# Stick-breaking attention by two sigmoids and a running product, with the scores read from PSUM

## What is computed

```python
z = jnp.einsum('bhqd,bhkd->bhqk', q_blk, kh).astype(jnp.float32) * inv_sqrt
mask = key_pos[None, :] < q_pos[:, None]
log_1m_beta = jnp.where(mask, jax.nn.log_sigmoid(-z), 0.0)
suffix = lax.cumsum(log_1m_beta, axis=3, reverse=True) - log_1m_beta
a = jnp.where(mask, jnp.exp(jax.nn.log_sigmoid(z) + suffix), 0.0)
return jnp.einsum('bhqk,bhkd->bhqd', a, vh.astype(jnp.float32)).astype(q.dtype)
```

## Time and profile before

| | us |
|---|---|
| median of three runs | 3073.14 |
| lowest, highest | 3069.12, 3074.96 |
| profiled execution | 3063.84 |
| its span | 3062.1 |
| stage of this attention, from 1864 to 2102 us | 238 |
| in it, PE, DVE and ACT busy | 200.3, 195.5, 137.0 |

### The profile page before, as it was taken

How to read it: one execution, slowest core, us unless ns; L and a number is a source line. 1 busy time by engine, 2 the same in 40 slices (tenths; PEclk the granted TensorE clock), 3 DMA queues, 4 the chain that set the end, 5 groups by cost and what they waited for, 6 DMA issues and landing times.

```text
span 3062.1 us, 42914 instructions
## 1 busy us (share of the span) xinstructions
PE 2875.2 (94%) x16394; PEld 2321.4 (76%) x16394; DVE 1624.6 (53%) x2005; ACT 752.3 (25%) x1421; POOL 1058.9 (35%) x746
## 2 busy tenths in 40 slices
PE   7998898979899999999799999879998999999997
PEld 6886567868788888888678886657876888888886
DVE  3464544662677777777732005884134455445545
ACT  3323564323311111101420004563124001100111
POOL 4321001348534333333643322112358333323333
PEclk9998999999999999999899999999999999999999
DMA  3200000013222222222221111001131111111111
GB/s 123 55 27 11 10 6 22 3 48 133 69 89 77 81 82 85 87 82 82 83 69 45 51 35 35 15 1 56 55 124 56 55 41 55 48 48 43 53 49 61
DMA packets 213435, 172.12 MB, mean 56 GB/s; under 512 B 15543, under 2 KB 188878, under 8 KB 213326
## 3 DMA queue, kind: packets, MB, share of 16 engines
q1 hardware_dynamic: 160670, 135.47, 14.3%
q10 hardware_dynamic: 52656, 35.13, 3.8%
HBM read 162.19 MB, written 8.39 MB: 56 GB/s over the span
## 4 chain that ended last, share of the span: by engine, by line
PE 82%; DVE 8%; POOL 4%; issue 2%; ACT 2%; DMA 1%; SPq 0%; DVEq 0%; ACTq 0%; POOLq 0%
PE ps L873 13%; PE ps L875 13%; PE ps L874 13%; PE ps L1290 7%; PE ps L1291 7%; PE ps L1292 7%; PE ps L1082 2%; PE ps L1000 2%; DVE sb_weights L2476 1%; PE ps L892 1%; PE ps L894 1%; PE ps L893 1%; POOL rstd L666 1%; PE ps L1022 1%; POOL slab_lo L240 1%
## 5 line engine op out<-in xcount | busy, mean ns | idle before, releaser
L237 POOL TENSOR_SCALAR slab_hi<-raw 128x1024 fp32r<-128x1024 f32 (+1 forms) x236 | 263.4, 1116 | 1540.4 <-PE ps L875 581.1
L240 POOL TENSOR_TENSOR slab_lo<-raw,slab_hi 128x1024 fp32r<-128x1024 f32 (+1 forms) x236 | 576.8, 2444 | 19.7
L873 PE MATMUL ps<-act_hi,slab_hi 128*128 128x512 f32 x1472 | 575.2, 391 | 2.0 <-DVE act_lo L1986 1.6
L875 PE MATMUL ps<-act_hi,slab_lo 128*128 128x512 f32 x1472 | 572.9, 389 | 0.0
L874 PE MATMUL ps<-act_lo,slab_hi 128*128 128x512 f32 x1472 | 572.7, 389 | 0.0
L2391 DVE TENSOR_TENSOR acc<-ps,acc 128x512 f32<-128x512 f32 x512 | 339.5, 686 | 200.6 <-PE ps L1292 200.5
L1290 PE MATMUL ps<-slab_hi,hid_hi 128*128 128x512 f32 x1024 | 403.4, 394 | 4.2 <-POOL acc L794 2.5
L1291 PE MATMUL ps<-slab_hi,hid_lo 128*128 128x512 f32 x1024 | 399.5, 390 | 0.0
L1292 PE MATMUL ps<-slab_lo,hid_hi 128*128 128x512 f32 x1024 | 399.3, 390 | 0.0
L1813 ACT ACTIVATE relu<-ps 128x512 f32<-128x512 f32 x128 | 77.0, 602 | 1041.2 <-PE ps L875 1023.1
L873 PEld LDWEIGHTS ps<-act_hi,slab_hi 128*128 128x128 f32 x1472 | 276.4, 188 | 59.8 <-DVE act_lo L1986 1.7
(11 more groups left out here) (320 smaller groups left out, 4252.9 us busy)
## 6 DMA issues: line engine op xcount, KB each, us to landing
raw<-in_w_in SPq DMA_DIRECT2D x56, 512.0 KB, 3.8
w_ada<-in_w_ada ACTq DMA_DIRECT2D x48, 512.0 KB, 4.1
raw<-in_w_out SPq DMA_DIRECT2D x32, 512.0 KB, 3.4
raw<-in_w_up SPq DMA_DIRECT2D x32, 512.0 KB, 4.1
raw<-in_w_down SPq DMA_DIRECT2D x32, 512.0 KB, 3.2
raw<-in_w_mlp_in SPq DMA_DIRECT2D x32, 512.0 KB, 4.1
raw<-in_w_mlp_out SPq DMA_DIRECT2D x32, 512.0 KB, 3.3
x_tok<-in_x SPq DMA_DIRECT2D x8, 512.0 KB, 6.2
```

The costliest lines, as they stand in the source:

```text
L237: pool.tensor_scalar(self.hi[s][:, 0:width], self.raw[r][:, 0:width], 1.0, 0.0, ALU.mult, ALU.add)\
L240: pool.tensor_tensor(self.lo[s][:, 0:width], self.raw[r][:, 0:width], self.hi[s][:, 0:width].bitcast(F32), ALU.subtract).then_inc(self.spl ...
L873: pe.matmul(o, hi[:, w], a_hi[:, k, cols], start=(k == 0), stop=False)
L875: mm = pe.matmul(o, lo[:, w], a_hi[:, k, cols], start=False, stop=(k == nk - 1))
```

## The change

The weights are computed as products instead of by logarithms. ACT reads the scores from PSUM twice: sigmoid(z) into sb_weights and sigmoid(-z) into a new tile sb_rest (two buffers, in the place of sb_z). DVE forms the running product of sb_rest from the last key to the first, and multiplies sb_weights by it, shifted by one key. The copies of the scores by DVE go. DVE adds -1e30 (0 below the diagonal) to the 128 columns on the diagonal, in place in PSUM, for both items of a tile behind the weights of an even item. The banks of the scores are free when ACT has read them (sb_beta_done). The turned weights are copied, without an exp. On PE the scores of the next tile move behind the transposes of item s - 2. The table of functions of ACT is another one, which has Tanh too.

```diff
@@ PE
-                pe.wait_ge(sem("sb_z_copied"), SB_ITEMS * i + 2 * t + 2)
+                pe.wait_ge(sem("sb_beta_done"), SB_ITEMS * i + 2 * t + 2)
...
-                    if s % 2 and s + 1 < SB_ITEMS:
-                        sb_scores(i, s // 2 + 1)
                     if s % 2 == 0 and s < 12 and not last:
                         sb_project(i + 1, s // 3, SB_THIRDS[s % 3])
                     if s % 2 == 0 and (late := lagged(i, before, s, SB_LAG_PV, SB_ITEMS)):
                         sb_outputs(late[0], late[1] // 2)
                     if late := lagged(i, before, s, SB_LAG_TURN, SB_ITEMS):
                         sb_turn(*late)
+                    if s % 2 and s + 1 < SB_ITEMS:
+                        sb_scores(i, s // 2 + 1)
                     if s % 2 and s < 12 and not last:
                         sb_project(i + 1, s // 3, SB_THIRDS[s % 3])
...
-            pe.wait_ge(sem("sb_z_copied"), SB_ITEMS * SB_PAIRS + 2)
+            pe.wait_ge(sem("sb_beta_done"), SB_ITEMS * SB_PAIRS + 2)
@@ ACT
-            act.preload_act_table_set("natural_log_exp_and_others")
+            act.preload_act_table_set("sigmoid_and_others")
...
-            def sb_softplus(i, s, before):
-                n = (s // 2 + 1) * P
-                z, l = sb_z[s % 2][:, 0:n], sb_w[s % SB_SLOTS][:, 0:n]
-                act.wait_ge(sem("sb_z_copied"), SB_ITEMS * i + s + 3)
+            def sb_betas(i, s, before):
+                n, at = (s // 2 + 1) * P, SB_ITEMS * i + s
+                z = ps[:, 2 * (s % 2):2 * (s % 2) + 2, :].rearrange("p b n -> p (b n)")[:, 0:n]
+                act.wait_ge(sem("sb_masked"), at + 1)
                 if slot := lagged(i, before, s, SB_SLOTS, SB_ITEMS):
                     act.wait_ge(sem("sb_turned"), SB_GROUPS * slot[0] + (sb_groups(slot[1])[-1] + 1))
-                act.activation(l, z, ACT.Exp).then_inc(sem("sb_exp_done"), 1)
-                act.wait_ge(sem("sb_exp_done"), SB_ITEMS * i + s + 1)
-                act.activation(l, l, ACT.Ln, bias=1.0).then_inc(sem("sb_ln_done"), 1)
+                act.activation(sb_w[s % SB_SLOTS][:, 0:n], z, ACT.Sigmoid)
+                if at >= 2:
+                    act.wait_ge(sem("sb_arg_done"), at - 1)
+                act.activation(sb_rest[s % 2][:, 0:n], z, ACT.Sigmoid, scale=-1.0).then_inc(sem("sb_beta_done"), 1)
...
-                    act.activation(sb_at[g % 4][:, 0:w], ps[:, 4 + g % 2, 0:w], ACT.Exp).then_inc(sem("sb_at_done"), 1)
+                    act.copy(sb_at[g % 4][:, 0:w], ps[:, 4 + g % 2, 0:w]).then_inc(sem("sb_at_done"), 1)
@@ DVE
+            def sb_mask(i, s):
+                f, col = divmod(s // 2 * P, HALF)
+                diagonal = ps[:, 2 * (s % 2) + f, col:col + P]
                 dve.wait_ge(sem("sb_scores"), SB_ITEMS * i + s + 1)
-                if n > P:
-                    dve.tensor_scalar(z[:, 0:n - P], scores[:, 0:n - P], SB_Z_CAP, None, ALU.min)
-                dve.tensor_tensor(z[:, n - P:n], scores[:, n - P:n], key_cap, ALU.min).then_inc(sem("sb_z_copied"), 1)
...
+                dve.tensor_tensor(diagonal, diagonal, consts[:, C_KEYCAP:C_KEYCAP + P], ALU.add).then_inc(sem("sb_masked"), 1)
+
+            def sb_weights(i, s):
+                n, at = (s // 2 + 1) * P, SB_ITEMS * i + s
+                rest, w = sb_rest[s % 2], sb_w[s % SB_SLOTS]
+                dve.wait_ge(sem("sb_beta_done"), at + 3)
+                ch.link(dve.tensor_tensor_scan(rest[:, 0:n][:, ::-1], rest[:, 0:n][:, ::-1], rest[:, 0:n][:, ::-1], 1.0, ALU.mult, ALU.bypass))
+                dve.tensor_tensor(w[:, 0:n - 1], w[:, 0:n - 1], rest[:, 1:n], ALU.mult).then_inc(sem("sb_arg_done"), 1)
```

More of the change, by code:

```diff
@@ L65 @@
 SB_LAG_TURN, SB_LAG_PV = 2, 4
-SB_Z_CAP = 40.0
+SB_MASKED = -1e30
 def sb_groups(s):
@@ L167, in constants @@
         c[:, C_LEVEL + n * CHUNK:C_LEVEL + (n + 1) * CHUNK] = ((k[:, :CHUNK] // s) % 2 == 1) & (r % CHUNK // s == k[:, :CHUNK] // s - 1)
-    c[:, C_KEYCAP:C_KEYCAP + P] = np.where(k < r, SB_Z_CAP, -1e30)
+    c[:, C_KEYCAP:C_KEYCAP + P] = np.where(k < r, 0.0, SB_MASKED)
     c[:, C_ID64:C_ID64 + CHUNK] = r % CHUNK == k[:, :CHUNK]
@@ L431, in two_blocks @@
         k2 = [sb(f"k2_feat{i}", kb, [P, SEQ]) for i, kb in enumerate((21, 85))]
-        sb_z = [sb(f"sb_z{i}", 41 + 4 * i, [P, SEQ]) for i in range(2)]
+        sb_rest = [sb(f"sb_rest{i}", 41 + 4 * i, [P, SEQ]) for i in range(2)]
         sb_w = [sb(f"sb_weights{i}", kb, [P, SEQ]) for i, kb in enumerate((49, 53, 73, 77))]
@@ L652, in _ @@
             for name, credit in (("kk_prod", 1), ("o_taken", 1), ("o_ss_done", 1), ("ada_used", 2), ("ada_read", 1), ("c2_cg_read", 1), ("c2_v_done", 1), ("c2_y_done", 1),
-                                 ("m_gate_read", 2), ("m_done", 2), ("sb_z_copied", 2), ("sb_o_done", 2)):
+                                 ("m_gate_read", 2), ("m_done", 2), ("sb_beta_done", 2), ("sb_o_done", 2)):
                 pool.sem_inc(sem(name), credit)
@@ L1930, in sb_pair @@
                         sb_take_projection(i + 1, s // 3 - 1)
-                    sb_softplus(i, s, before)
+                    sb_betas(i, s, before)
                     if late := lagged(i, before, s, SB_LAG_TURN, SB_ITEMS):
@@ L2458, in _ @@
                         .then_inc(sem("m_done"), 1)
-            key_cap = consts[:, C_KEYCAP:C_KEYCAP + P]
-            def sb_cap_scores(i, s):
-                n = (s // 2 + 1) * P
-                z, scores = sb_z[s % 2], ps[:, 2 * (s % 2):2 * (s % 2) + 2, :].rearrange("p b n -> p (b n)")
+            def sb_mask(i, s):
+                f, col = divmod(s // 2 * P, HALF)
+                diagonal = ps[:, 2 * (s % 2) + f, col:col + P]
                 dve.wait_ge(sem("sb_scores"), SB_ITEMS * i + s + 1)
-                if n > P:
-                    dve.tensor_scalar(z[:, 0:n - P], scores[:, 0:n - P], SB_Z_CAP, None, ALU.min)
-                dve.tensor_tensor(z[:, n - P:n], scores[:, n - P:n], key_cap, ALU.min).then_inc(sem("sb_z_copied"), 1)
@@ L2472, in sb_log_weights @@
-            def sb_log_weights(i, s):
-                n = (s // 2 + 1) * P
-                z, l = sb_z[s % 2][:, 0:n], sb_w[s % SB_SLOTS][:, 0:n]
-                dve.wait_ge(sem("sb_ln_done"), SB_ITEMS * i + s + 1)
-                ch.link(dve.tensor_tensor_scan(l[:, ::-1], l[:, ::-1], l[:, ::-1], 0.0, ALU.add, ALU.bypass))
-                dve.wait_ge(sem("sb_z_copied"), SB_ITEMS * i + s + 3)
-                dve.tensor_tensor(l, z, l, ALU.subtract).then_inc(sem("sb_arg_done"), 1)
-                dve.wait_ge(sem("sb_arg_done"), SB_ITEMS * i + s + 1)
@@ L2481, in _ @@
-            sb_cap_scores(0, 0)
+                dve.tensor_tensor(diagonal, diagonal, consts[:, C_KEYCAP:C_KEYCAP + P], ALU.add).then_inc(sem("sb_masked"), 1)
[5 more added lines that the diff above has]
+                dve.tensor_tensor(w[:, 0:n - 1], w[:, 0:n - 1], rest[:, 1:n], ALU.mult).then_inc(sem("sb_arg_done"), 1)
@@ L2482, in _ @@
+            sb_mask(0, 0)
+            sb_mask(0, 1)
             for i in range(SB_PAIRS):
                 for s in range(SB_ITEMS):
-                    if s + 1 < SB_ITEMS:
-                        sb_cap_scores(i, s + 1)
-                    elif i + 1 < SB_PAIRS:
-                        sb_cap_scores(i + 1, 0)
-                    sb_log_weights(i, s)
+                    sb_weights(i, s)
+                    if s % 2 == 0:
+                        for h in range(2):
+                            if s + 2 < SB_ITEMS:
+                                sb_mask(i, s + 2 + h)
+                            elif i + 1 < SB_PAIRS:
+                                sb_mask(i + 1, h)
```

## The result

The changed kernel takes 3082.8 us (median of seven runs, 3077.7 to 3086.9); the kernel before, run beside it on the same chip, 3069.5 (3064.7 to 3075.0). The ratio is 1.004, with a 95% interval of 1.0027 to 1.0053 (8 to 16 us): slower by 13 us. The profiled executions are 3082.2 and 3063.8 us, 18 apart; that of the kernel before is shorter than all of its seven runs, so differences read from this pair of traces may be some us too large.

The account below looks back on a forecast made before the run. PE was taken to bound tiles 0 to 4 of a pair, DVE tiles 5 to 7 and the last pair. Stage +14.8, GpSimd 0.5 and clock 0.8 gave +16: 3089 us on the median, range 3075 to 3106.

Parts of the forecast that it names:

- The round trip: Attention tiles: PE transposes 2t-2, ACT copies it, ACT does two sigmoids, PE scores; stalls sum to 11.6 us a pair.
- Its price: Projecting pairs: stall per tile 0.99 us at t=1 growing to 2.34 at t=7, plus 1.2 for projection copies.
- The last pair: Last head pair, without projections: tile periods 3.6 to 7.5 us, about 37.0 against 41.1, so -4.1 us.
- The clock: TensorE's grant behind long waits at a pair's end: about +0.4 us for each of two boundaries, 0.8 in all.
- The clock rival: Projecting tiles: new stalls lower the grant, eight stretches, 32 us less half for what lies in stalls; 3105 us, chance 0.08.
- The stage: Stick-breaking attention: pairs +7.1, +6.1, +5.7 and -4.1 us, tail 0, sum +14.8.
- From the profiled time to the median: Whole kernel: +16 us on the profiled 3063.8 gives 3080, on the median 3073.1 gives 3089.
- slow scan: DVE's product scan at 1.5 times the adding scan exceeds the round trip in wide tiles: +13, 3102 us, chance 0.04.
- DVE's relief: Attention stage: 56 capped copies, 38.7 us, go; DVE is busy 30 to 35 us less and no longer bounds the first three pairs.
- The faster case: Attention pairs: the round trip is covered and only DVE's relief is left; -20 us, 3053, chance 0.06.
- T: PE's transposes of item 2t-1, the only PE work forecast to cover the round trip; 0.26 us at t=1, 0.92 at t=7.
- rival of half stalls: Attention tiles: the two sigmoids may overlap, stalls are half the sum, no change; about 3074 us, chance 0.10.

Follow-up runs that it names:

- e_act: Changed kernel with ACT doing both items' sigmoids of a tile first, then the copies of both turned items; 3071.3 us, ratio 1.0005 to the kernel before.
- e_proj: Changed kernel with the next pair's projections at odd items put ahead of the next tile's scores on PE; 3068.9 us, ratio 0.9995 to the kernel before.
- e_odd: Changed kernel with sigmoid(z) done twice for each odd item, 20.4 us more of ACT; 3117.8 us, ratio 1.0163 to the kernel before.
- e_even: Changed kernel with sigmoid(z) done twice for each even item, 20.4 us more of ACT; 3096.8 us, ratio 1.0092 to the kernel before.
- e_fill: Changed kernel with four spare matmuls before tile 5's scores in each projecting pair; median ratio 1.004 to the kernel before.
- e_dve: Changed kernel with 56 DVE reductions, 38.7 us, in the removed copies' widths, results unawaited; 3089.5 us, ratio 1.007 to the kernel before.
- e_outfill: Changed kernel with projections ahead of scores, outputs between a tile's transposes, and eight spare matmuls at item 13 of projecting pairs; 3062.0 us, ratio 0.9981 to the kernel before.
- e_back: Changed kernel with PE's order of the kernel before, scores ahead of the transposes of item 2t-1; 3112.4 us, ratio 1.0139 to the kernel before.
- e_bmove: Kernel before with only PE's new order, next tile's scores behind the transposes of item 2t-1; 3075.1 us, ratio 1.0014 to the kernel before.

## Why the prediction was right, and where its steps were off

Forecast were 3089 us and slower; it is 3083 and slower, by 13 us where 16 were forecast. The rest of the distance is the kernel before, whose median was 3073.1 us in the three runs that the forecast started from and 3069.5 in seven. Step by step:

- **The round trip** is the cause, as forecast. e_act takes ACT's copies out of it and e_proj puts PE's work under it; either removes the loss. e_odd against e_even shows that an activation costs over twice as much inside it as outside (16.9 us of idle PE against 7.2).
- **Its price** was well summed, but not as the steps had it. In the first pair PE's waits before the scores are 1.30, 1.02, 1.32, 1.93, 0.76, 0.97 and 0.54 us. Up to tile 5 they follow the forecast (0.99, 1.20, 1.42, 1.62, plus 0.6 twice for a projection's copy). Then they fall instead of growing beyond 2: an item of over 512 columns is turned in two groups, and PE waits for ACT's copies or for DVE between the transposes (0.66, 0.83 and 1.93 us), so part of the trip is paid there, though the kernel before had a wait of 2.4 us for DVE in the last of these places too. Together 11.3 us, where 12.8 were forecast; the waits before scores alone are 7.8, not the 9 to 12 that I had named as the sign.
- **Why less:** two activations in a row overlap, the two sigmoids of an item by 0.10 to 0.17 us, 0.12 in the mean of 64. In the timeline above they start 0.58 us apart and last 0.71. I had taken durations where the starts' distance counts, and allowed some 0.05. My remark that by the Trainium skill's figure the sum would move under 1 us was wrong. Put into the same steps, the figure of the Trainium skill (ScalarE: Activation LUTs, What ACT_TABLE_LOAD costs) adds 0.65 us to a projecting pair and 0.8 to the last, near 3 us in all (an estimate from the page's figure).
- **The last pair** was forecast at 37.0 and took 34.9. The periods from scores to scores at 384 to 1024 columns are 3.25, 4.08, 4.72, 5.56, 6.30 and 7.05 us, each 0.3 to 0.5 under the step's. Three to four such overlaps in a tile would give as much (an estimate; it was not tested apart).
- **The clock** is the mis-sized term. I gave it 0.4 us at each of two boundaries, 0.8 in all. The idle time of the projecting pairs was a little under the forecast, but PE's busy time rose by 3.3 (2.3 without the eight transposes that moved into the window), 2.6 and 2.0 us where I had added nothing but the 0.8. e_fill is 1.6 to 2.1 us a pair shorter, some 5 in all; in its third pair the stretch at the pair's end is missing too. The clock rival had named the mechanism, falls within the projecting tiles, but with eight stretches and a price of 32 us less half; there were three, at 1.6 to 2.1. Three is in part chance: in e_dve and e_even the same wait was followed by a fall once in three pairs each.
- **The stage** comes to +17.8 us against +14.8: projecting pairs 2.1, 2.2 and 0.8 longer than forecast, the last one 2.1 shorter. The errors are +5.1 and -2.1 us, and 3.0 remain; with the 1.3 us that I had added for GpSimd and the clock, the stage is off by 1.7.
- **From the profiled time to the median:** I carried the difference between the profiled executions over to the medians. It was 18 us between two single executions and 13 by the medians, and the stage of the kernel before from which I took every difference belongs to an execution that was faster than all of its seven runs. Part of the closeness is luck: the right stage difference, 17.8, put on the median by the same step gives 3091, farther from 3083 than the forecast.
- **Right as taken:** the scan's rate (slow scan, 3102: no), the sigmoid's rate, DVE's relief (159.0 us busy in the five windows against 193.4, in the 30 to 35 forecast), the table loads worth nothing (tail 17.9 in both), the mask in place. GpSimd still blocks DVE, a scan of 512 columns taking 3.21 us during its pass, as in the earlier trace rows; what that costs now was not measured apart.
- **The faster case** fell as argued: PE has nothing but T to cover the trip. e_dve shows that of the 29 us of DVE's relief in the projecting pairs 3 us show in their length, or 5 in PE's idle time. The overlap on which the rival of half stalls rested is there, 0.12 us, but it takes about 1.5 us from a pair's 12.8 and not half.

## What to carry to other kernels

When a buffer changes its reader, write down the loop that its release closes: here PE's scores came to depend on ACT, whose queue held a copy that depends on PE. Such a loop costs its whole length less what stands between its ends on each engine, whatever the engines' busy shares say, and here it was mended by order alone (work moved under it, or the coupling instruction behind it). Price each activation of a run by the distance between starts; and where a change adds waits of PE, give the range a term for the work behind them at half clock: here it came behind some waits of 1.9 to 2.6 us and not behind others of the same length.

## What the runs showed of the hardware beyond what was expected

- **A short wait has a long price.** Behind the waits of 1.93 and 2.59 us above, PE's next scores took 2.93 and 3.35 us instead of 1.56 and 1.99, and whole pairs were 1.4 to 2.1 us longer than with the gap filled. Whether the grant falls behind a given wait is not settled by the wait's length: behind 1.93 us it didn't in four of six pairs of e_dve and e_even, and behind 1.05 us in e_even's last pair it did (scores 2.93 us). e_outfill, with its longest wait filled, is the one kernel whose grant is 1.00 in all five windows.
- **A loop with PE idle in each tile can stay at half clock.** In e_back's last pair it did for 20 us on end at a grant of 0.50; with four spare matmuls a tile the whole pair's was 1.00, and the pair 8 us shorter for more work.
- **The tail depends on it too.** The merge gate's stretch takes 17.9 us at a grant of 1.00 and 19.5 at 0.91, in e_act, e_proj, e_even, e_odd and e_dve (19.3 at 0.92 in e_bmove), though PE's work in it is the same.
- **A running product costs what a running sum does,** 2282 and 2283 ns at 1024 columns. A pass of DVE in place in PSUM took 294 ns at 128 columns.
